# Two-block transformer kernel: the 16-byte lines of the activation chunks rearranged into 64-byte runs, and the split weight tiles moved against them

## The reference

```
first block:  h = rmsnorm(x); z = h @ w_in -> conv branch, attention with forget gates, two sigmoid gates
              x += (gate_c * conv_branch + gate_a * attn_branch) @ w_mix_out
              x += square(relu(rmsnorm(x) @ w_ff1)) @ w_ff2          (width 8192); x = rmsnorm(x)
second block: mod = silu(c) @ w_ada + b_ada                          (six vectors)
              h = rmsnorm(x) * (1 + scale) + shift; h @ w_in -> attention with position bias, state-space mixer
              x += gate * (concat(attn, ssm) @ w_out)
              x += gate * ((silu(g) * v) @ w_down), g, v = conv(h @ w_up)   (width 2 x 5632); x = rmsnorm(x)
```

## Time and profile before

| what | value |
|---|---|
| median of 3 runs | 2445.82 us (2445.46 to 2445.92) |
| span of the profiled execution | 2444.7 us, that is 1.1 us below the median |
| PE busy | 2423.8 us, 99% |
| DVE busy | 1969.0 us, 81% |
| ACT busy | 1261.4 us, 52% |
| bytes moved | 566.81 MB, mean 232 GB/s |
| matmul instructions | 14373 |

### The profile page before, as it was taken

The page is one execution under the profiler, slowest core; times in us unless marked ns, Lnnn a source line. Parts: engine busy times, 40 slices in busy tenths (PEclk is TensorE's granted clock), DMA queues, the critical chain, the costliest instruction groups (busy, mean ns, idle before and its releaser), DMA issues.

```text
span 2444.7 us, 47745 instructions
## 1 busy us (share of the span) xinstructions
PE 2423.8 (99%) x14373; PEld 2149.2 (88%) x14373; DVE 1969.0 (81%) x3114; ACT 1261.4 (52%) x2038; POOL 89.1 (4%) x109
## 2 busy tenths in 40 slices
PE   8999999999999999999999999999999999999998
PEld 7888888888888888888888988889888888888887
DVE  7778876689987887887898877776887887887886
ACT  6444445565554454554555555565545445445455
POOL 0000001000000000000000105300000000000000
PEclk9999999999999999999999999999999999999999
DMA  7786885657888888888888555555566656656555
GB/s 275 274 282 211 279 284 192 200 190 268 285 292 293 287 291 292 286 293 291 289 288 281 175 177 194 188 171 190 167 187 200 202 180 198 198 178 212 192 176 169
DMA packets 162812, 566.81 MB, mean 232 GB/s; under 512 B 18883, under 2 KB 19452, under 8 KB 162748
## 3 DMA queue, kind: packets, MB, share of 16 engines
q1 hardware_dynamic: 132572, 458.71, 56.4%
q10 hardware_dynamic: 27792, 101.20, 12.5%
q0 software_dynamic: 2384, 6.09, 1.0%
HBM read 563.51 MB, written 2.42 MB: 231 GB/s over the span
## 4 chain that ended last, share of the span: by engine, by line
PE 77%; DVE 4%; issue 2%; ACT 1%; DVEq 0%; DMA 0%; ACTq 0%; SPq 0%
PE bank L334 77%; DVE w_lo L1345 1%; DVE scratch L1994 0%; DVE scratch L1992 0%; DVE scratch L1351 0%; DVE scratch L1997 0%; ACT w_hi L823 0%; DMA w_raw<-in_w_in 0%; DVE Z L1705 0%; DVE H L1714 0%; DVE scratch L2020 0%; ACT U L1297 0%; DVE scratch L2014 0%; DVE scratch L1378 0%; PE bank L678 0%
## 5 line engine op out<-in xcount | busy, mean ns | idle before, releaser
L1345 DVE TENSOR_TENSOR w_lo<-w_raw,w_hi 128x1024 fp32r<-128x1024 f32 (+2 forms) x898 | 1048.0, 1176 | 117.1 <-ACT w_hi L823 107.5
L334 PE MATMUL bank<-H,w_hi 128*128 128x512 f32 (+1 forms) x4480 | 1100.0, 386 | 9.3 <-ACT w_hi L275 8.1
L334 PEld LDWEIGHTS bank<-H,w_hi 128*128 128x128 f32 x4480 | 799.3, 188 | 136.7 <-issue 11.2
L823 ACT ACTIVATE w_hi<-w_raw 128x1024 fp32r<-128x1024 f32 (+2 forms) x898 | 876.4, 1012 | 24.1 <-PE bank L334 8.4
L334 PEld LDWEIGHTS bank<-H,w_lo 128*128 128x128 f32 x4416 | 591.5, 188 | 40.5
L334 PE MATMUL bank<-H,w_lo 128*128 128x256 f32 x4416 | 602.9, 277 | 0.0
L334 PE MATMUL bank<-U,w_hi 128*128 128x512 f32 (+1 forms) x2011 | 501.7, 384 | 0.5 <-DVE U L2022 0.3
L853 ACT ACTIVATE scratch<-bank 128x256 f32<-128x256 f32 x355 | 135.1, 381 | 669.3 <-PE bank L334 668.7
L334 PEld LDWEIGHTS bank<-U,w_hi 128*128 128x128 f32 x2011 | 351.1, 188 | 50.0 <-DVE U L2022 0.6
L334 PEld LDWEIGHTS bank<-U,w_lo 128*128 128x128 f32 x1984 | 275.3, 188 | 23.7
L334 PE MATMUL bank<-U,w_lo 128*128 128x256 f32 x1984 | 282.1, 277 | 0.0
(11 more groups left out here) (246 smaller groups left out, 1113.2 us busy)
## 6 DMA issues: line engine op xcount, KB each, us to landing
w_raw<-in_w_ff SPq DMA_DIRECT2D x256, 512.0 KB, 5.0
ada_w<-in_w_ada ACTq DMA_DIRECT2D x192, 512.0 KB, 4.7
w_raw<-in_w_up SPq DMA_DIRECT2D x176, 512.0 KB, 4.5
w_raw<-in_w_z SPq DMA_DIRECT2D x96, 512.0 KB, 4.8
w_raw<-in_w_in SPq DMA_DIRECT2D x88, 512.0 KB, 4.4
w_raw<-in_w_gate SPq DMA_DIRECT2D x64, 512.0 KB, 4.6
w_raw<-in_w_down SPq DMA_DIRECT2D x64, 384.0 KB, 3.2
w_raw<-in_w_down SPq DMA_DIRECT2D x64, 320.0 KB, 3.4
```

The costliest lines, as they stand in the source:

```text
L334: return nc.tensor.matmul(out, lhsT, rhs, start=start, stop=stop, skip_group_check=True)
L823: A(w_hi[:, slot, 0:cols], w_raw[:, slot, 0:cols], ACT.Copy).then_inc(sem("w_high"), 1)
L1345: TT(w_lo[:, slot, 0:cols], w_raw[:, slot, 0:cols], w_hi[:, slot, 0:cols].bitcast(F32), ALU.subtract)\
```

## The change

The halves of a chunk are laid out in another order. A chunk is a block of 2048 bytes of its own again. It is cut into 16 strips of 128 bytes; the first 64 bytes of a strip belong to the high half and the next 64 bytes to the low half. Element order within a half is by rounds: round 0 takes the first 32 bytes (a pair of lines) of each of the 16 strips, round 1 the second 32 bytes; rounds 2 and 3 do the same for the low half. A matmul of 512 columns makes four rounds, one of 256 columns two.

`w_hi` and `w_lo` get 7 and 15 lines of padding ahead of them, so that both stand 13 lines behind the chunks modulo 16 (256 bytes). `R` and `ss` move into the gap between `H` and `U`. The scalar_tensor_tensor instructions that write low halves become two for a chunk, one for each round, since their access pattern has a dimension more; the attention chunks' tensor_tensor is done for each chunk alone.

```diff
-STEP = 3
-LINES = 2 * T // LINE
-CHAIN_N = NC * 2 * T + (STEP - 1) * 2 * T
+RUN = 8
+ROUNDS = 4
+SWEEP = 2 * T // ROUNDS // RUN
+AREA_N = NC * 2 * T
+GAP = 1024
+HIGH_AT, LOW_AT = 7, 15
...
-        def chunks_by_line(name, at):
-
-            area = nc.alloc_sbuf_tensor_at(name, [P, CHAIN_N], F32R, offset=base + at)
-            return bass.AP(area[:, :].tensor, LINE, [[CHAIN_N, P], [2 * T, NC], [STEP * LINE, LINES], [1, LINE]])
...
+        def chunks_in_rounds(name, at):
+
+            area = nc.alloc_sbuf_tensor_at(name, [P, AREA_N], F32R, offset=base + 4 * at)
+            return area[:, :].rearrange("p (k i a e) -> p k a i e", k=NC, a=ROUNDS, e=RUN)
...
-        w_hi = sb("w_hi", [P, 4, PIECE], F32R)
-        w_lo = sb("w_lo", [P, 4, PIECE], F32R)
+        w_hi, w_lo = (sb(name, [P, LINE * at + 4 * PIECE], F32R)[:, LINE * at:].rearrange("p (s c) -> p s c", s=4)
+                      for name, at in (("w_hi", HIGH_AT), ("w_lo", LOW_AT)))
...
-        R = sb("R", [P, T])
-        ss = sb("ss", [P, T])
+        R = nc.alloc_sbuf_tensor_at("R", [P, T], F32, offset=base + 4 * AREA_N)
+        ss = nc.alloc_sbuf_tensor_at("ss", [P, T], F32, offset=base + 4 * (AREA_N + T))
...
         def lines(ap):
-            return ap.rearrange("p (l e) -> p l e", e=LINE)
+            return ap.rearrange("p (a i e) -> p a i e", i=SWEEP, e=RUN)
...
+            def low_rounds(out, full, scalar, high, op):
+
+                for a in range(ROUNDS // 2):
+                    last = STT(out[:, a, :, :], lines(full)[:, a, :, :], scalar, high[:, a, :, :].bitcast(F32), op, ALU.subtract)
+                return last
...
-                    STT(ob(H, k, 1), lines(zb(16 + k)), mod[:, shift + k:shift + k + 1], ob(H, k, 0).bitcast(F32),
-                        ALU.add, ALU.subtract).then_inc(sem("h_ready"), 1)
+                    low_rounds(ob(H, k, 1), zb(16 + k), mod[:, shift + k:shift + k + 1], ob(H, k, 0), ALU.add)\
+                        .then_inc(sem("h_ready"), 1)
...
-                TT(B[:, 8 + h:8 + h + n, LINES // 2:LINES, :], attn_out[:, h:h + n, :].rearrange("p n (l e) -> p n l e", e=LINE),
-                   B[:, 8 + h:8 + h + n, 0:LINES // 2, :].bitcast(F32), ALU.subtract)\
-                    .then_inc(sem("out2.operand"), n)
+                for k in range(h, h + n):
+                    TT(ob(B, 8 + k, 1), lines(attn_out[:, k, :]), ob(B, 8 + k, 0).bitcast(F32), ALU.subtract)\
+                        .then_inc(sem("out2.operand"), 1)
```

More of the change, by code:

```diff
@@ L107, in build @@
         base = (nc.sbuf_base + 31) // 32 * 32
-        ctx.enter_context(nc.sbuf_tensor("arena", [P, 3 * NC * 2 * T + 1024 + (Z_BLOCKS - 32) * T], F32))
+        ctx.enter_context(nc.sbuf_tensor("arena", [P, 3 * AREA_N + GAP + (Z_BLOCKS - 32) * T], F32))
         def sb(name, shape, dt=F32):
@@ L118, in sem @@
             return sems[name]
-        def chunks_by_line(name, at):
-            area = nc.alloc_sbuf_tensor_at(name, [P, CHAIN_N], F32R, offset=base + at)
-            return bass.AP(area[:, :].tensor, LINE, [[CHAIN_N, P], [2 * T, NC], [STEP * LINE, LINES], [1, LINE]])
[L126 to L132, removed]
+        def chunks_in_rounds(name, at):
+            area = nc.alloc_sbuf_tensor_at(name, [P, AREA_N], F32R, offset=base + 4 * at)
+            return area[:, :].rearrange("p (k i a e) -> p k a i e", k=NC, a=ROUNDS, e=RUN)
+        H = chunks_in_rounds("H", 0)
+        U = chunks_in_rounds("U", AREA_N + GAP)
+        B = chunks_in_rounds("B", 2 * AREA_N + GAP)
+        G = nc.alloc_sbuf_tensor_at("G", [P, NC, 2, T], F32, offset=base + 4 * (AREA_N + GAP))
+        Z = nc.alloc_sbuf_tensor_at("Z", [P, Z_BLOCKS, T], F32, offset=base + 4 * (2 * AREA_N + GAP))
         X = sb("X", [P, NC, T])
@@ L233, in lines @@
         def lines(ap):
-            return ap.rearrange("p (l e) -> p l e", e=LINE)
+            return ap.rearrange("p (a i e) -> p a i e", i=SWEEP, e=RUN)
         def whole(buf, k):
-            return buf[:, k, :, :]
+            return buf[:, k, :, :, :]
         def ob(buf, i, part):
-            at = slice(part * LINES // 2, (part + 1) * LINES // 2)
+            at = slice(part * ROUNDS // 2, (part + 1) * ROUNDS // 2)
             if isinstance(i, int):
-                return buf[:, i, at, :]
-            return buf[:, bass.ds(i, 1), at, :].rearrange("p a l e -> p (a l) e")
+                return buf[:, i, at, :, :]
+            return buf[:, bass.ds(i, 1), at, :, :].rearrange("p k a i e -> p (k a) i e")
         def gates(m, par):
@@ L1412, in _ @@
                     dve.wait_ge(sem("h_high"), k + 1)
-                    STT(ob(H, k, 1), lines(X[:, k, :]), V("g_mix", k), ob(H, k, 0).bitcast(F32), ALU.mult, ALU.subtract)\
-                        .then_inc(sem("h_ready"), 1)
+                    low_rounds(ob(H, k, 1), X[:, k, :], V("g_mix", k), ob(H, k, 0), ALU.mult).then_inc(sem("h_ready"), 1)
                 if i < 2:
@@ L1619, in _ @@
                     dve.wait_ge(sem("mix.x"), m + 1)
-                    STT(ob(H, m, 1), lines(xb(m)), V("g_mlp", m), ob(H, m, 0).bitcast(F32), ALU.mult, ALU.subtract)\
-                        .then_inc(sem("h_ready"), 1)
+                    low_rounds(ob(H, m, 1), xb(m), V("g_mlp", m), ob(H, m, 0), ALU.mult).then_inc(sem("h_ready"), 1)
                     add_square("mix", par, m)
```

## The result

The changed kernel takes 2463.76 us (median of 4 runs, 2462.42 to 2466.21), the kernel before 2445.64 us beside it (4 runs, 2444.95 to 2445.92). The ratio is 1.0076 (95% interval 1.0063 to 1.0088): 18 us slower, where 2401 us was forecast.

What follows compares the result with a forecast made beforehand. The matmuls' own pace on TensorE was taken as the bound. From the profile's 2444.7 us, − 49 for reading order and + 4 for VectorE gave a span of 2400, so a median of 2401 us; range 2350 to 2490.

Steps and rivals of the forecast that it cites:

- What bounds the kernel: Whole kernel: only the matmuls' own pace and about 21 us of idle PE set the time; matmuls sum to 2320 us.
- 1 ns on every matmul is worth some 14 us: Whole kernel: a nanosecond on each long matmul is worth 6.8 us, one on each short matmul 6.9 us.
- At half clock nothing besides the columns: Second block's start: at 1.2 GHz, 256-column matmuls take 213.6 ns, the columns' 213.3 and nothing besides; should stay at 213.
- The place of the weight tiles, 0: Weight tiles going from 11 to 3 lines ahead of the chunks: no row for the new position, taken as 0.
- The row of `narrow`: Matmuls with 16-column weight loads: distance 227.5 ns, 3 ns longer than with full loads, taken as showing that place matters.
- The order of reading, − 49 us: Long and short matmuls: jumps halve, so half the loss goes, 4.5 and 2.6 ns each, 31 + 18 = 49 us.
- `keep_warm`'s contiguous reading: Fourth matmul of `keep_warm`, without jumps: 5 to 10 ns more than the long form; opposite bound, 82 us slower.
- The rule of lines: Matmul reads: each new 16-byte line costs, 128 lines stay, so pace stays 224.8 and 114.3 ns; rival, 2450 us, chance 0.15.
- most of the loss goes with the moving lines and not with the weights: Long matmuls: the second 256 columns lose 3.8 ns for 64 moving lines though the weight load can be over.
- VectorE, + 4 us: Low halves on VectorE, two instructions for one: 0.155 us more a chunk; + 4 us on the path, bounds 1 and 9.
- the slower rival: Matmul reads: round 0 returns to only 4 of 16 line positions, so pays more often; 2491 us, chance 0.24.
- All the loss goes: Matmul reads: collisions of the two read streams avoided by the right distance, − 96 us; 2358 us, chance 0.25.

Runs made afterwards that it cites:

- old order at place 3: Kernel before with padding that moves the weight tiles by 8 lines, to start 3 lines ahead of the chunks modulo 16 instead of 11: 2511.46 us, ratio 1.0271.
- (12, 12): Changed kernel without its padding, high and low weight tiles both starting 12 lines ahead of the chunks modulo 16: 2528.32 us, ratio 1.0342.
- (3, 3): The changed kernel itself, high and low weight tiles both starting 3 lines ahead of the chunks modulo 16: 2463.76 us, ratio 1.0076.
- (0, 9): Changed kernel with high weight tile 0 and low one 9 lines ahead of the chunks modulo 16 (padding 4 and 9): 2437.38 us, ratio 0.9971.
- bare matmuls of the step order: Network left out, only matmuls on chunks with lines three apart, weight tiles at 16 starts, loads of 128 to 16 columns: 227.4 ns mean at 128, 223.7 at 16.
- place 11: Weight tiles starting 11 lines past the chunk modulo 16, as in the kernel before; matmuls alone, group of 16: 2741 ns for pairs, 2706 for lines three apart.
- bare grid: Network left out, eight long and eight short matmuls, three times per pair of weight-tile starts (16 x 16); lines three apart: 2706 to 2787 ns; pairs average 2789.
- (5, 5): Changed kernel with both weight tiles 5 lines ahead of the chunks modulo 16 (padding 9 and 15): 2436.91 us, ratio 0.9963; matmuls alone: 2666 ns a group.
- pairs at place 5: Network left out, long matmuls on the new order's chunk, weight tile starting 5 lines past it modulo 16: settled at 220, 228.5 or 240 ns.

## Why the prediction was wrong

- *What bounds the kernel*: right. The matmuls' own pace set the time before and after. That 1 ns on every matmul is worth some 14 us holds roughly: with the old order at place 3 a group takes 88 ns more, 5.5 ns a matmul, and the kernel 66 us, 12 for each.
- *At half clock nothing besides the columns*: right, 213.3 ns again.
- *The place of the weight tiles, 0*: this term failed first. Moving both tiles by 8 lines in the old order cost 66 us, and in the new one (12, 12), (3, 3) and (0, 9) are 2528, 2464 and 2437 us. The prediction said that it had no row for the new place, and then gave a term without a row the value nothing. With ± 65 us for it, the forecast would have had no sign.
- The row of `narrow` (227.5 ns) from which it took that the place matters at all did not show that much. With 16 columns and a fixed place the bare matmuls of the step order take 223.2 to 224.6 ns at every place. `narrow` also changes its place from one matmul to the next, and its single distances go up and down between 222 and 232 ns. The conclusion was right and its ground weak.
- *The order of reading, − 49 us*: this step failed too, as a rule. It took the loss (9.0 and 5.1 ns) as proportional to the number of jumps and as independent of the place. Long and short matmuls at 220 and 111.7 ns were forecast; at the place chosen the main cycle has 225.4 and 115.5 on average, and the second one 231 and 116.4. The same new order gives 220, 225, 232 or 240 ns by its place and by the cycle it is in, and the old one 224.5 to 232.5. The averages over all places even go against the jumps: 227.4 ns with 127 of them, 230.1 with 63, 232.0 with none. The prediction had the sign of this in hand, in `keep_warm`'s contiguous reading that was 5 to 10 ns slower, and used it only as a bound. The rule of lines in the Trainium skill ("SBUF — State Buffer", "Specifications (TRN2)") gave an unchanged pace, and these differences at an unchanged 128 lines are not in it either.
- *How the terms add up.* Place first and then order, the kernels give + 66 and − 51 us and + 3 for VectorE, which is the 18 measured to within 1 us. The − 51 beside a forecast of − 49 is luck: at place 3 the long distance fell from 232.5 to 225.4 ns, not from 224.8 to 220, and at place 11 the bare matmuls give the new order a loss. Neither order nor place has a value of its own; they act together, and with the phase in which a piece begins. The old layout stood at the best place of the bare grid with a perfectly even pace. A steady distance in every row of before could have been read as a sign of that: a change would more likely leave such a place than find a better one.
- *That most of the loss goes with the moving lines and not with the weights*: right for the step order. Of about 14 ns over the columns some 4 go when the weight load shrinks from 128 to 16 columns, and 10 stay.
- *VectorE, + 4 us*: right, 3.2 us by its own experiment. The helper's line 1341 now stands for the old lines 1413, 1620 and 1714. The weight loads waited 1.6 us for line 1413 and 0.6 for line 1620; now they wait 5.1 us for the helper:

```profile
L339 PEld LDWEIGHTS bank<-H,w_hi 128*128 128x128 f32 x4480 | 800.3, 188 | 146.0 <-issue 11.4 <-DVE H L1341 5.1 <-ACT w_hi L828 0.4
```

- *The rivals*: the measured 2464 us lies within the range of 2350 to 2490, but only because the slower rival (chance 0.24) was in it. Its sign was right, but its mechanism (round 0 comes back to four positions too soon) isn't what was found: the same round 0 makes the fastest group of all at (5, 5). Its size, 2491, was too large. "All the loss goes" happens nowhere; the lowest steady distances seen are 220 and 113 ns.
- The sum by the measured terms: 16.3 us from the groups and 3.2 us from VectorE, 19.5, for 19.6 between the two profiled executions and 18.1 between the medians.

## What to carry to other kernels

Where fp32r matmuls run back to back at full clock, the offset modulo 256 bytes between the weight tiles and the moving operand is worth trying out: over the places run here it changed the kernel's time by 2.7% in the one order and 3.7% in the other, for at most some 350 bytes of padding, and no simple rule was found. A series of bare matmuls over all places, before the kernel is touched, shows which places are worth a run. For pairs it gave the kernel's pace to 1 ns at four places; for lines three apart, with the chunk one line off the kernel's start, it did not. So the bare chunk should start where the kernel's does, and each place should be entered from more than one state. Don't judge a new access order at one place alone, and don't take the best place of a bare series for granted: it can have a second, slower cycle. An unexplained loss of a few ns per instruction is not yet a loss that goes with the number of jumps. A term for which there is no row needs a price with both signs, not a zero.

## What the runs showed of the hardware

- The distance of long fp32r matmuls (512 columns, 213.3 ns of them) at 2.4 GHz is 220 to 240 ns on average over a cycle, by access order, by place modulo 16 lines and by what went before; of short ones (106.7 ns) 113 to about 122. At 1.2 GHz (granted clock 0.50) it is 213.3 to 213.6 ns for 256 columns in both layouts, and nothing is lost.
- One configuration has several steady cycles: pairs at place 5 ran at 220, 228.5 and 240 ns. In the kernel, a cycle lasts until the next pause or change of operands, up to some 170 us.
- Moving the weights by 16 lines changes nothing; moving chunk and weights together by 5 lines does (220, 230 and 225 ns where 227, 220 and 230 stood).
- With lines three apart, weight loads of 16 instead of 128 columns reduce the spread over the places from 224.4 to 230.0 ns down to 223.2 to 224.6. In pairs they don't (226.5 to 240.1 ns), and some places get slower (6.00 us for 24 matmuls at place 5, against 5.72 or 5.56 with full loads).
- Fewer jumps do not mean a quicker matmul: 227.4 ns on average with lines three apart, 230.1 with pairs, 232.0 side by side.
